# The feed-forward output of a two-block transformer kernel: token tiles outside for the last four row blocks, norm and store by tile, another order of the weight chunks

## The reference

```
def swiglu(h, w_in, w_out):
    a, b = jnp.split(h @ w_in, 2, axis=-1)
    return (jax.nn.silu(a) * b) @ w_out
...
        h = rms_norm_2(x, norm_ffn_g[l])
        x = x + swiglu(h, ffn_in_w[l], ffn_out_w[l])
    return rms_norm_2(x, final_norm_g)
```

## Time and profile before

| what | value |
|---|---|
| median of 3 runs | 2175.74 us (2173.33 to 2180.53) |
| the profiled execution, own time | 2177.37 us |
| its span (first to last instruction) | 2175.5 us |
| busy PE, of the span | 1898.2 us, 87% |
| busy DVE, ACT, POOL | 660.3, 584.1, 624.0 us |
| mean granted PE clock, as a share of full | 0.94 |
| chain that ended last | PE 69%, DMA 17%, DVE 6%, ACT 4%, POOL 2%, issue 2% |

### The profile page before, as it was taken

How to read it: one execution, slowest core, us unless ns; L and a number is a source line. 1 busy time by engine, 2 the same in 40 slices (tenths; PEclk the granted TensorE clock), 3 DMA queues, 4 the chain that set the end, 5 groups by cost and what they waited for, 6 DMA issues and landing times.

```text
span 2175.5 us, 21286 instructions
## 1 busy us (share of the span) xinstructions
PE 1898.2 (87%) x8472; PEld 1226.0 (56%) x8472; DVE 660.3 (30%) x1369; ACT 584.1 (27%) x1042; POOL 624.0 (29%) x361
## 2 busy tenths in 40 slices
PE   4999979588778788739999999888899889999997
PEld 3544337333222222228888868544687568888886
DVE  6551265601010011044898024466211211000001
ACT  3113452110000000032232243556243423222211
POOL 0002223300000000034442234555355324555542
PEclk8998999789999899969997998999999999999999
DMA  9453201779999999952322322000233122232221
GB/s 373 155 227 130 92 0 64 307 323 416 428 428 428 429 427 428 388 187 78 116 78 78 97 78 88 24 25 21 95 119 116 39 71 76 96 98 96 87 107 58
DMA packets 94306, 379.22 MB, mean 174 GB/s; under 512 B 6235, under 2 KB 35291, under 8 KB 79884
## 3 DMA queue, kind: packets, MB, share of 16 engines
q1 hardware_dynamic: 88048, 356.47, 42.1%
q0 software_dynamic: 3456, 12.58, 1.5%
q10 hardware_dynamic: 2716, 8.98, 1.0%
HBM read 357.50 MB, written 20.51 MB: 174 GB/s over the span
## 4 chain that ended last, share of the span: by engine, by line
PE 69%; DMA 17%; DVE 6%; ACT 4%; POOL 2%; issue 2%; SPq 0%; DVEq 0%; ACTq 0%; POOLq 0%
DMA slots<-in_w_expert_up 15%; PE bank L717 14%; PE bank L719 14%; PE bank L718 14%; PE bank L692 11%; PE bank L1029 7%; PE bank L1227 2%; PE bank L1207 1%; PE bank L845 1%; ACT area L1727 1%; POOL low_r L2439 1%; DMA slots<-in_w_ada 1%; PE bank L763 1%; PE bank L1050 1%; PE bank L1196 1%
## 5 line engine op out<-in xcount | busy, mean ns | idle before, releaser
L2439 POOL TENSOR_TENSOR low_r<-slots,high_r 128x2048 fp32r<-128x2048 f32 x87 | 401.0, 4611 | 603.0 <-ACT high_r L1411 603.0
L718 PE MATMUL bank<-xl_r,high_r 128*128 128x512 f32 (+1 forms) x864 | 330.0, 382 | 0.0
L717 PE MATMUL bank<-area_r,high_r 128*128 128x512 f32 x800 | 313.7, 392 | 1.3 <-POOL low_r L2439 1.3
L1029 PE MATMUL bank<-slots,area 128*64 128x512 f32 x992 | 252.6, 669 | 71.0 <-DMA slots<-in_w_expert_gate 36.5
L719 PE MATMUL bank<-area_r,low_r 128*128 128x512 f32 x800 | 311.8, 390 | 0.0
L1411 ACT ACTIVATE high_r<-slots 128x2048 fp32r<-128x2048 f32 x87 | 166.4, 1915 | 440.1 <-PE bank L719 417.2
L1029 PEld LDWEIGHTS bank<-slots,area 128*64 128x64 f32 x992 | 77.5, 152 | 245.5 <-issue 154.6
L718 PEld LDWEIGHTS bank<-xl_r,high_r 128*128 128x128 f32 x864 | 162.9, 189 | 31.7 <-issue 0.5
L717 PEld LDWEIGHTS bank<-area_r,high_r 128*128 128x128 f32 x800 | 150.7, 188 | 32.7 <-POOL low_r L2439 1.5
L719 PEld LDWEIGHTS bank<-area_r,low_r 128*128 128x128 f32 x800 | 150.6, 188 | 31.7
L2265 DVE SCALAR_TENSOR_TENSOR bank<-area,cols,bank 128x512 f32<-128x512 f32 x232 | 153.5, 761 | 0.0
(11 more groups left out here) (378 smaller groups left out, 2688.1 us busy)
## 6 DMA issues: line engine op xcount, KB each, us to landing
slots<-in_w_expert_up SPq DMA_DIRECT2D x32, 2048.0 KB, 19.6
slots<-in_w_expert_down SPq DMA_DIRECT2D x32, 2048.0 KB, 19.6
slots<-in_w_expert_gate SPq DMA_DIRECT2D x30, 2048.0 KB, 18.3
slots<-in_w_in SPq DMA_DIRECT2D x15, 2048.0 KB, 8.8
slots<-in_w_ada SPq DMA_DIRECT2D x11, 2048.0 KB, 12.2
slots<-in_ffn_in_w SPq DMA_DIRECT2D x22, 1024.0 KB, 6.6
slots<-in_ffn_out_w SPq DMA_DIRECT2D x5, 2048.0 KB, 7.9
slots<-in_w_out SPq DMA_DIRECT2D x4, 2048.0 KB, 8.5
```

The lines of the kernel that those rows point to most:

```text
L717: nc.tensor.matmul(out, xh, yh, start=start and n == 0, stop=False)
L718: nc.tensor.matmul(out, xh, yl, start=False, stop=False)
L1029: last = nc.tensor.matmul(banks[which][piece, :], XT[b][:, k, piece], w[side][:, k, :], start=k == 0, stop=k == KT - 1)
L2439: nc.gpsimd.tensor_tensor(low_half(m), raw_half(m), high_half(m), ALU.subtract).then_inc(s["w_low"], 1)
```

## The change

FFOUT becomes [4, 4, 4, 2, 4, 4]: the chunk with two row blocks is now the fourth of six. PE keeps the old loop for row blocks 0 to 17. For the last four, 18 to 21, it first waits for both pieces of the last chunk, and then goes over the token tiles and halves outside, with the four row blocks inside: each bank gets 12 matmuls in a row and is then complete. To have both pieces at once, the high part of the very last piece is written to the upper half of xl_r, which holds no live data once the input projection is over, so ACT's wait for it is on the end of that projection.

The norm goes by tile and by half. DVE adds a half to X and multiplies it by the gain into XO; ACT squares the half with a sum; DVE turns the first half's sum into a bias, and ACT's Sqrt takes the second half's sum with that bias; DVE takes the reciprocal; ACT multiplies the first half of the tile by it and DVE the second half. SP stores the tile from XO. There are two new semaphores, x_gained and rstd_ready.

```diff
--- before.py
+++ after.py
@@ -116,7 +116,7 @@
 plan("xq", ["act"] * 8, 2)
 plan("xo", ["dve"] * 8, 2)
 plan("ffin", ["act", "act", "dve", "dve"] * (FT // 2), FT // 2, 2)
-FFOUT = [4, 4, 4, 4, 4, 2]
+FFOUT = [4, 4, 4, 2, 4, 4]
 
 
 def emptied(engine, g):
...
@@ -265,6 +265,8 @@
             return slot(slot_of(c))[:, half * n:(half + 1) * n]
 
         def high_half(m):
+            if m == len(HALVES) - 1:
+                return xl_r[:, 2048:4096]
             return high_r[:, m % 2 * 2048:m % 2 * 2048 + HALVES[m][2]]
 
         def low_half(m):
@@ -405,6 +407,10 @@
         GT = A(8432, FT * C, FT)
         SA = A(19696, 2048, 4)
         FG2 = A(4096, D)
+        XO = A(0, 4096, TT)
+        SQO = [A(19696 + i * C, C) for i in range(4)] + [slot(3)[:, i * C:(i + 1) * C] for i in range(4)]
+        half_ssq, last_bias, last_std, last_rstd = (small[:, 224:232], small[:, 232:236], small[:, 236:240],
+                                                    small[:, 240:244])
 
         g_dram = dram("bias_falling", [NH, NG])
         h2_dram = dram("h2_rows", [S, D])
@@ -664,8 +670,8 @@
                 chunk(CHUNK_NO["ffout"] + n, [(0, ffout[:, k0:k0 + k, :])])
                 k0 += k
             for t in range(TT):
-                sp.wait_ge(s["x_final"], TT + t + 1)
-                sp.dma_start(io["out"][0, t * P:(t + 1) * P, :], X[:, t, :]).then_inc(s["out_done"], 16)
+                sp.wait_ge(s["x_final"], TT + 2 * t + 2)
+                sp.dma_start(io["out"][0, t * P:(t + 1) * P, :], XO[:, t, :]).then_inc(s["out_done"], 16)
             sp.wait_ge(s["out_done"], 16 * TT)
 
 
@@ -1323,20 +1329,29 @@
                     last.then_inc(s["proj_done"], 1)
             all_emptied(FIRST["ffin"] + 2 * FT)
             split_emptied("ffn")
-            for f in range(FT):
+            def ffn_out(f, t, half, w):
+
+                tokens, out_cols = slice(t * P, (t + 1) * P), slice(half * C, (half + 1) * C)
+                return split_product(banks[2 * t + half][:, :],
+                                     [(GTH[f][:, tokens], GTL[:, f, tokens], w[0][:, f % 2, out_cols],
+                                       w[1][:, f % 2, out_cols])], start=f == 0, stop=f == FT - 1)
+
+            for f in range(FT - 4):
                 if f % 2 == 0:
-                    wh, wl = parts(FIRST_HALF["ffout"] + f // 2, 2)
+                    w = parts(FIRST_HALF["ffout"] + f // 2, 2)
                     pe.wait_ge(s["tile_low"], 3 * KT + f + 2)
                 for t in range(TT):
                     for half in range(2):
-                        tokens, out_cols = slice(t * P, (t + 1) * P), slice(half * C, (half + 1) * C)
-                        last = split_product(banks[2 * t + half][:, :],
-                                             [(GTH[f][:, tokens], GTL[:, f, tokens], wh[:, f % 2, out_cols],
-                                               wl[:, f % 2, out_cols])], start=f == 0, stop=f == FT - 1)
-                        if f == FT - 1:
-                            last.then_inc(s["ff_full"], 1)
-                if f % 2 == 1 and f < FT - 1:
+                        last = ffn_out(f, t, half, w)
+                if f % 2 == 1:
                     last.then_inc(s["ff_used"], 1)
+            w = [parts(len(HALVES) - 2, 2), parts(len(HALVES) - 1, 2)]
+            pe.wait_ge(s["tile_low"], 3 * KT + FT)
+            for t in range(TT):
+                for half in range(2):
+                    for f in range(FT - 4, FT):
+                        last = ffn_out(f, t, half, w[(f - FT + 4) // 2])
+                    last.then_inc(s["ff_full"], 1)
 
 
         @block.scalar
@@ -1404,7 +1419,9 @@
                 while highs[0] < upto_half:
                     m = highs[0]
                     c, half = HALVES[m][:2]
-                    if m >= 2:
+                    if m == len(HALVES) - 1:
+                        act.wait_ge(s["proj_done"], FIRST["ffin"] + 2 * FT)
+                    elif m >= 2:
                         act.wait_ge(s[HALVES[m - 2][3]], HALVES[m - 2][4])
                     if half == 0:
                         act.wait_ge(w_loaded[slot_of(c)], loaded_value(c))
@@ -1808,7 +1825,20 @@
                 split_weights(FIRST_HALF["ffin"] + 2 * j + 4)
             split_products(FT // 2 - 1)
             split_weights(len(HALVES))
-            norm(A(0, 4096, TT), s["x_ff"], 1)
+            k = norms[0]
+            for t in range(TT):
+                for half in range(2):
+                    act.wait_ge(s["x_ff"], 2 * t + half + 1)
+                    nc.scalar.activation(SQO[2 * t + half], X[:, t, half * C:(half + 1) * C], ACT.Square,
+                                         accum_out=half_ssq[:, 2 * t + half:2 * t + half + 1]
+                                         ).then_inc(s["ssq_ready"], 1)
+                act.wait_ge(s["ssq_ready"], TT * k + 2 * t + 2)
+                act.wait_ge(s["var_ready"], k + t + 1)
+                nc.scalar.activation(last_std[:, t:t + 1], half_ssq[:, 2 * t + 1:2 * t + 2], ACT.Sqrt,
+                                     bias=last_bias[:, t:t + 1], scale=1.0 / D).then_inc(s["std_ready"], 1)
+                act.wait_ge(s["rstd_ready"], t + 1)
+                nc.scalar.activation(XO[:, t, 0:C], XO[:, t, 0:C], ACT.Copy, scale=last_rstd[:, t:t + 1]
+                                     ).then_inc(s["x_final"], 1)
 
 
         @block.vector
@@ -2413,10 +2443,23 @@
                 for half in range(2):
                     dve.wait_ge(s["ff_full"], 2 * t + half + 1)
                     piece = slice(half * C, half * C + C)
-                    ins = nc.vector.tensor_tensor(X[:, t, piece], banks[2 * t + half][:, :], X[:, t, piece], ALU.add)
-                ins.then_inc(s["x_ff"], 1)
-            dve.wait_ge(s["fg2_loaded"], 16)
-            final_norm(FG2)
+                    nc.vector.tensor_tensor(X[:, t, piece], banks[2 * t + half][:, :], X[:, t, piece], ALU.add
+                                            ).then_inc(s["x_ff"], 1)
+                    if t == half == 0:
+                        dve.wait_ge(s["fg2_loaded"], 16)
+                    dve.wait_ge(s["x_ff"], 2 * t + half + 1)
+                    nc.vector.tensor_tensor(XO[:, t, piece], X[:, t, piece], FG2[:, piece], ALU.mult
+                                            ).then_inc(s["x_gained"], 1)
+                    if half == 0:
+                        dve.wait_ge(s["ssq_ready"], TT * norms[0] + 2 * t + 1)
+                        nc.vector.tensor_scalar(last_bias[:, t:t + 1], half_ssq[:, 2 * t:2 * t + 1], 1.0 / D, EPS,
+                                                ALU.mult, ALU.add).then_inc(s["var_ready"], 1)
+                dve.wait_ge(s["std_ready"], norms[0] + t + 1)
+                dve.wait_ge(s["x_gained"], 2 * t + 2)
+                nc.vector.reciprocal(last_rstd[:, t:t + 1], last_std[:, t:t + 1]).then_inc(s["rstd_ready"], 1)
+                dve.wait_ge(s["rstd_ready"], t + 1)
+                nc.vector.tensor_scalar(XO[:, t, C:2 * C], XO[:, t, C:2 * C], last_rstd[:, t:t + 1], None, ALU.mult
+                                        ).then_inc(s["x_final"], 1)
 
 
         @block.gpsimd
```

More of the change, by code:

```diff
@@ L198 @@
               "nsa_out", "nsa_kept", "mem_loaded", "x_full", "x_scored", "x_exp", "x_rcp", "x_probs", "x_t_full",
-              "x_t_ready", "x_out", "x_kept", "ff_used", "ff_full", "x_ff", "fg2_loaded", "router_loaded", "zeros_set", "zeros_stored", "h2_ready", "h2_stored", "pool_step", "router_exp_in", "router_exp_out", "onehot_ready",
+              "x_t_ready", "x_out", "x_kept", "ff_used", "ff_full", "x_ff", "x_gained", "rstd_ready", "fg2_loaded", "router_loaded", "zeros_set", "zeros_stored", "h2_ready", "h2_stored", "pool_step", "router_exp_in", "router_exp_out", "onehot_ready",
               "ctl_ready", "gate_full", "up_full", "down_full", "xt_full", "xt_ready", "silu_ready",
```

## The result

| | median, us | ratio to before, 95% interval |
|---|---|---|
| before | 2175.74 (7 runs, 2173.33 to 2180.53) | |
| changed | 2186.74 (7 runs, 2181.45 to 2188.88) | 1.0043 [1.003, 1.0055] |

The change makes the kernel 0.43% slower. Its profiled execution took 2183.54 us with a span of 2181.7, 6.2 over that of before. The output projection began 1.4 us earlier in it, for reasons far ahead of the change, so the two traces are best compared from the first matmul of the output projection to the end of the span: 2175.5 - 2041.29 = 134.2 us before, 2181.7 - 2039.87 = 141.8 after, +7.6.

What follows compares the result with a forecast made beforehand. PE's count of matmuls was taken to bound the kernel until the last one, then a tail of 11.94 us. Stalls 12.0 + clock 4.4 - order 0.4 - new end 5.9 = +10.1 us, giving 2185.8 us; range 2181 to 2190.

Steps and rivals of the forecast that it cites:

- first late chunk: Output projection: PE waits 3.7 us ahead of row block 14, for a load issued after row block 11.
- second late chunk: Output projection: PE waits 8.3 us ahead of row block 18, for a load issued after row block 15 and both pieces.
- clock after the first: After the stall ahead of row block 14, PE comes back at the lower clock; 2.2 us lost.
- clock after the second: After the stall ahead of row block 18, PE comes back at the lower clock; 2.2 us lost.
- matmuls for a bank in a row: Last 96 matmuls of the output projection, twelve in a row for each bank: 21.8 us in place of 22.2, gain 0.4.
- the new end: Tail after the last matmul, norm by tile and half: 6.07 us in place of 11.94, gain 5.9.
- The rival of one stall alone: Output projection: only the first load late, the last chunk's load going out after row block 13; -0.1 us, 2175.6, chance 0.03.
- the one without any: Output projection: no load is late and the change does what it says; -6.0 us, 2169.7, chance 0.03.
- rival 3: Only the first stall; ahead of row block 18 PE waits 0.3 us for POOL's second piece; 2175.6 us, chance 0.03.
- the two prices in the prediction: Expert groups of 32 matmuls after 3.79 to 3.88 us idle: five lost 1.7 us, four 2.6 to 2.9.
- rivals 1 and 2: Both stalls; lower clock after only one (+7.9 us, 2183.6, chance 0.12), or after neither (+5.7, 2181.4, chance 0.08).
- Five terms of six: Tail's parts: add 0.72, square 0.75, Sqrt 0.28, reciprocal 0.21, half multiplies 0.72, store and end 3.39 us.

Runs made afterwards that it cites:

- E2: The kernel before with nothing but the new chunk order [4, 4, 4, 2, 4, 4]; 2185.08 us, ratio 1.0038 to the kernel before.
- E1: The changed kernel with the old chunk order [4, 4, 4, 4, 4, 2]; 2173.37 us, ratio 0.9972 to the kernel before.
- E3: The changed kernel, with each load waiting for the pieces really there (7 in place of 8 for the last chunk); 2175.96 us, ratio 0.9991.
- E4: The changed kernel with 32 matmuls of a zero operand ahead of the wait for the last chunk; 2186.23 us, ratio 1.0038.
- E6: The changed kernel with old chunk order and old loop over row blocks to the end, keeping the new end; 2181.54 us, ratio 1.0014.
- E7: The changed kernel with old chunk order and the old end (one norm for all tiles), keeping the new loop; 2177.19 us, ratio 1.0003.

## Why the prediction was right, and where its terms were off

The direction and the cause were right: two late loads and the lower clock outweigh the new end. +10.1 us was forecast, and the medians differ by 11.0. That these are so near to each other is in part luck: the terms seen in the traces add up to less. Term by term, on the profiled execution:

| term | forecast, us | changed kernel | where shown |
|---|---|---|---|
| first late chunk | +3.7 | +3.2 | E2 has it without the tile order, E1 removes it |
| second late chunk | +8.3 | +7.8 | E3: 7.65 us of idle time become 0.23 |
| clock after the first | +2.2 | 0 in this profile, 1.6 in E2, E3, E4 | slow matmuls counted |
| clock after the second | +2.2 | +2.7 | E4 removes it |
| matmuls for a bank in a row | -0.4 | 0 | last 96 in 22.3 us with no wait (E1, E3) |
| the new end | -5.9 | -6.1 | E6, E7: only both together |
| sum | +10.1 | +7.6 | |

**The late chunks.** The reading of the wait's formula held for both. Each came out 0.5 us shorter, mostly for one reason: the loads landed after 7.4 and 7.6 us, where I took 7.9; POOL's pieces were 4.5 us and not 4.6. The first idle time goes with its load from run to run: 2.98 us where it landed after 7.4 (the changed kernel and E3), 3.17 after 7.6 (E2), 3.57 after 8.0 (E4). The rival of one stall alone, and the one without any, are refuted by the timeline. E3 separates the two parts of the second: at most 7.4 us hang on the counted wait, 0.2 on POOL's second piece once the load is early (rival 3 had put 0.3 on it).

**The clock.** This is where a single profile does not settle the number. After some 3 us of idle time the clock fell in four cases (E2 twice, E3, E4) and stayed once (the changed kernel's profile); each fall at this length cost 1.6 us, near the lower of the two prices in the prediction, 1.7. After 7.65 us it cost 2.7. The changed kernel's profiled execution is the one without the first fall and is also the second fastest of its seven; with a fall it would have a stage 9.2 us longer than before. That the other executions, and with them the median of +11.0, do have it is likely, but their traces were not taken, and the runs of this kernel differ among themselves by 7 us. A slower load may be in it as well, 0.6 us of the first stall if it lands as late as in E4. Neither is shown, so why the median lies 3.4 us beyond the 7.6 of the trace stays open, as far as it is not the scatter of the runs: the interval of the ratio is 6.5 to 12.0 us.

The nine groups of the earlier trace rows could not say what follows an idle time of 3 us, since all of theirs were 3.79 us or longer. The kernel before has shorter ones too: one of 2.37 us that the clock did not outlast, and groups of the same 32 matmuls where it goes both ways (timeline of PE; 7.09 us is the group at full clock, 8.78 has lost 1.7):

```profile
520.68 7.09 PE L1029 MATMUL bank<-slots,area 128*64 128x512 f32 x32 [2.55 <-DMA slots<-in_w_expert_gate]
...
786.71 7.09 PE L1029 MATMUL bank<-slots,area 128*64 128x512 f32 x32 [2.20 <-DMA slots<-in_w_expert_up]
...
850.41 8.78 PE L1029 MATMUL bank<-slots,area 128*64 128x512 f32 x32 [2.21 <-DMA slots<-in_w_expert_up]
```

So the rows of the kernel before left it open what follows a stall of 3 us, between the lengths that went both ways and those that always lost. The nine of nine that the prediction holds against rivals 1 and 2 speaks for stalls as long as theirs, here the second.

**The order of matmuls.** This term was wrong: I gave the order of the banks a gain of 0.4 us, and the runs show none. I took 2.72 us for twelve matmuls from the cross-attention output, that is 0.227 for each, and ascribed the difference to the 0.231 us of the output projection to the change of banks. With twelve matmuls in a row for a bank and no wait between, the last 96 take 22.42 us in E1 from first start to last end, or 22.26 without the 0.16 us by which the last one outlasts its turn: 0.232 for each, as before. Changing banks every three matmuls costs nothing here. What makes matmuls of the output projection 2% slower than those of cross-attention stays open.

**The end.** Five terms of six were within 0.08 us. The store and what is behind it took 3.06 us and not 3.39, so the tail is 5.8 us and not 6.1.

## What to carry to other kernels

A wait that counts pieces as "two for each chunk" is right only while all the chunks before the last are of one size; with a short chunk moved forward, every wait that counts past it asks for more than it needs. Here it was one wait, for 8 pieces in place of 7, and since it asks for too much it shows as time and not as a wrong result. Even with exact counts a short chunk shortens the cover of the next load: with two slots, a load has only the chunk between to hide in, and 11.1 us of matmuls did not cover 14 us of load, split and remainder. At the end of a kernel, the loop order and the norm by tile are one change: a norm by tile needs banks that become complete one after the other (E6 without them is slower), and the reordered loop needs an end that makes use of them (E7 without it gains nothing).

## What the runs showed of the hardware that was not expected

An idle time of 2.98 us, the same to 0.01 us, was followed by the full clock in one execution and by 1.2 GHz over nine matmuls in another (changed kernel, E3); in one execution of the kernel before the same goes for 2.20 and 2.21 us. After 3.0 to 3.6 us the clock fell 0.8 to 1.5 us after PE had started again (E2, E3, E4), after 7.65 us PE started at 1.2 GHz. Matmuls of one shape had a steady pace of 0.227 us in the cross-attention output and 0.231 in the feed-forward output, both at a granted clock of 1.00; in the latter the order of the banks made no difference. The same load of 1024 KB landed 4.8 us after its issue in the kernel before and 5.6 us after it in E1.
